# Two output norms that give their rate behind the projection, a sum of squares on GpSimd, and a re-stepped preparation of RWKV

## The reference, cut to what matters

```
h = x
y_ssm = _s5_group(u, ...)          # ends in y * sigmoid(y @ w_glu + b_glu), y = gelu(...)
y_mla = _mla_group(...)            # 8 heads of softmax attention, o of width 1024
y = concatenate([_rmsnorm(y_ssm, ssm_out_norm_w), _rmsnorm(y_mla, mla_out_norm_w)])
h = h + y @ w_out
h = h + _conv_ffn(_rmsnorm(h, ffn_norm_w), ...)
# second layer, RWKV-7 part, before the scan
kk = k * k_k;  kk = kk / max(sqrt(sum(kk * kk, per head)), 1e-12)
k = k * (1 + (a - 1) * k_a)
# _rmsnorm(y, w) = y * rsqrt(mean(y * y) + eps) * w
```

## Time and profile before

| | us |
|---|---|
| median of 3 runs | 3262.21 (3261.06 to 3263.58) |
| the profiled execution | 3260.85 |
| its span | 3258.3 |
| PE busy | 2999.6 (92%) |
| DVE busy | 2159.4 (66%) |
| ACT busy | 1560.1 (48%) |
| POOL busy | 661.4 (20%) |

### The profile page before, as it was taken

One profiled execution on the slowest core, in us unless ns is written; L12 is line 12 of the kernel. 1 busy time (PEld: TensorE's weight loads), 2 busy tenths in 40 slices (PEclk: granted clock), 3 DMA queues, 4 the chain that ended last, 5 costly groups with the idle time before them and its releaser, 6 DMA issues.

```text
span 3258.3 us, 49703 instructions
## 1 busy us (share of the span) xinstructions
PE 2999.6 (92%) x19690; PEld 2659.3 (82%) x19690; DVE 2159.4 (66%) x3555; ACT 1560.1 (48%) x2542; POOL 661.4 (20%) x829
## 2 busy tenths in 40 slices
PE   5876899999999997899999999898899999999998
PEld 4864778888888887888888888776788888888887
DVE  8787778775777656766666666665666665566655
ACT  3334455554555544455555555444544444344443
POOL 5234102110112000764444440000100111001100
PEclk8987999999999998999999999998999999999999
DMA  4410445556555554322222223432364555655554
GB/s 180 152 65 23 159 143 185 190 175 192 203 194 188 166 176 162 127 72 85 82 85 84 73 82 101 154 112 78 130 203 172 191 186 174 194 201 192 193 167 144
DMA packets 78804, 475.13 MB, mean 146 GB/s; under 512 B 8113, under 2 KB 11185, under 8 KB 37425
## 3 DMA queue, kind: packets, MB, share of 16 engines
q1 hardware_dynamic: 76480, 459.66, 41.4%
q10 hardware_dynamic: 2096, 12.32, 1.1%
HBM read 465.66 MB, written 6.29 MB: 145 GB/s over the span
## 4 chain that ended last, share of the span: by engine, by line
PE 75%; DVE 14%; ACT 6%; issue 2%; POOL 2%; DMA 1%; DVEq 0%; ACTq 0%; SPq 0%
PE bank L684 35%; PE bank L688 22%; PE bank L686 4%; PE bank L687 4%; DVE m L1165 3%; ACT m L1979 2%; PE bank L700 2%; DVE m L1809 1%; PE bank L977 1%; POOL m L2599 1%; POOL m L2603 1%; PE bank L978 1%; PE bank L865 1%; PE bank L974 1%; PE bank L980 1%
## 5 line engine op out<-in xcount | busy, mean ns | idle before, releaser
L688 PE MATMUL bank<-m,m 128*128 128x256 f32 x6864 | 1939.7, 283 | 0.0
L684 PE MATMUL bank<-m,m 128*128 128x512 f32 x4992 | 1757.3, 396 | 17.1 <-POOL m L2478 10.2
L1165 DVE TENSOR_TENSOR m<-m,m 128x1024 fp32r<-128x1024 f32 (+1 forms) x944 | 1077.1, 1149 | 630.6 <-ACT m L1979 616.5
L688 PEld LDWEIGHTS bank<-m,m 128*128 128x128 f32 x6864 | 1311.5, 191 | 1.6
L1979 ACT ACTIVATE m<-m 128x1024 fp32r<-128x1024 f32 (+1 forms) x944 | 912.5, 979 | 786.0 <-PE bank L688 734.8
L684 PEld LDWEIGHTS bank<-m,m 128*128 128x128 f32 x4992 | 941.0, 189 | 231.1 <-issue 14.6
L686 PE MATMUL bank<-m,m 128*128 128x256 f32 x1872 | 573.7, 306 | 77.7 <-DVE m L1165 68.8
L687 PE MATMUL bank<-m,m 128*128 128x256 f32 x1872 | 541.1, 289 | 0.0
L686 PEld LDWEIGHTS bank<-m,m 128*128 128x128 f32 x1872 | 370.4, 198 | 107.5 <-issue 89.2
L687 PEld LDWEIGHTS bank<-m,m 128*128 128x128 f32 x1872 | 371.1, 198 | 3.3 <-issue 1.9
L2580 POOL TENSOR_TENSOR m<-m,m 128x256 fp32r<-128x256 f32 x44 | 63.4, 1441 | 695.6 <-ACT m L2180 695.6
(11 more groups left out here) (361 smaller groups left out, 3018.0 us busy)
## 6 DMA issues: line engine op xcount, KB each, us to landing
m<-in_w_up SPq DMA_DIRECT2D x88, 1024.0 KB, 4.9
m<-in_w_down SPq DMA_DIRECT2D x128, 704.0 KB, 4.0
m<-in_w_gu SPq DMA_DIRECT2D x88, 1024.0 KB, 4.9
m<-in_w_out SPq DMA_DIRECT2D x48, 1024.0 KB, 5.1
m<-in_w_krv SPq DMA_DIRECT2D x48, 1024.0 KB, 4.9
m<-in_w_xbc SPq DMA_DIRECT2D x24, 1024.0 KB, 4.9
m<-in_w_z SPq DMA_DIRECT2D x16, 1024.0 KB, 4.9
m<-in_w_in SPq DMA_DIRECT2D x14, 1024.0 KB, 5.0
```

The costliest lines, as they stand in the source:

```text
L684: pe.matmul(bank.rearrange("p (a b) -> p a b", a=2), hi, x, start=kc == L.k0, stop=False)
L688: m = pe.matmul(ps, lo, x[:, 0, :], start=False, stop=last)
L1165: v.tensor_tensor(lo_of(k), raw_of(k)[0], hi_of(k).bitcast(F32), SUB).then_inc(*lo_v(("lo", k)))
```

## The change

1. The norms of the heads (`N_mla`) and of the state space (`N_ssm`) become `late`: ACT cuts weight·chunk high, DVE low; DVE's `rated` multiplies each output tile by the rate (into `xb3`) and adds it to h, two DVE instructions as before. POOL squares and adds the chunks (`sum_squares`), inside the heads and inside GLU, and PE sums over the partitions once (`add_total`). L_out and L_out2 are no longer wide.
2. `o` and `vt` change places in h, and x comes back in two loads of 1 MB, h[:, 0:8] and h[:, 8:16].
3. Seven of the eight cuts of y go into L_out's odd tiles, and all low parts of y to POOL.
4. S5's setup: PE's transposes and k0 products, and ACT's copies of them, stand earlier.
5. RWKV's `prep` has seven steps instead of five or six: the exponentials are a step apart, the root comes ahead of `ka`, `spread`, DVE's `ka` product and DVE's last step are later, and one of the two empty rounds between the preparation and the solve goes.

```diff
@@ -448,8 +450,8 @@
-        o = h[:, 0:8, :]
-        vt = h[:, 8:16, :].rearrange("p (a b) c -> p a (b c)", a=2)
+        o = h[:, 8:16, :]
+        vt = h[:, 0:8, :].rearrange("p (a b) c -> p a (b c)", a=2)
@@ -556,9 +558,9 @@
-        L_out = linear("w_out", 16, 16, TWO, lambda t: res_v["mla", t], k0=8, wide=True)
+        L_out = linear("w_out", 16, 16, TWO, lambda t: res_v["mla", t], k0=8)
...
-        L_out2 = linear("w_out", 16, 16, FOUR, lambda t: res_v["ssm", t], k1=8, wide=True)
+        L_out2 = linear("w_out", 16, 16, FOUR, lambda t: res_v["ssm", t], k1=8)
@@ -604,9 +606,10 @@
-        N_mla = Norm(norms, [o[:, i, :] for i in range(8)], ("mla_out_norm_w", 0), hn_out[8:16], 1024, 1e-6, 2)
+        N_mla = Norm(norms, [o[:, i, :] for i in range(8)], ("mla_out_norm_w", 0), hn_out[8:16], 1024, 1e-6, 2,
+                     late=True)
...
-                     [(ssr[:, 0, i, :], ssr[:, 1, i, :]) for i in range(8)], 1024, 1e-6, 7)
+                     [(ssr[:, 0, i, :], ssr[:, 1, i, :]) for i in range(8)], 1024, 1e-6, 6, late=True)
@@ -623,6 +626,10 @@
+        def total_of(N):
...
+            return sqb if N is N_mla else (spare, xb3[2])
@@ -704,6 +711,11 @@
+            def add_total(N):
+                pe.wait_ge(*(mla_g if N is N_mla else glu_g)["sum", 7])
+                pe.matmul(banks[N.bank][:, 0:T], ones, total_of(N)[0], start=True, stop=True).then_inc(
+                    *sum_pe((N.id,)))
@@ -718,7 +730,7 @@
-                for _ in range(7):
+                for _ in range(5):
@@ -727,7 +739,7 @@
                             m.then_inc(*s5_pe(("abT", r, c // 4)))
-                for _ in range(6):
+                for _ in range(5):
                     yield
@@ -893,8 +905,10 @@
                 yield
+                yield
                 pe.wait_ge(*wkv_a["rn", i])
                 spread(b, rn4[e]).then_inc(*wkv_pe(("rn", i)))
+                yield
                 yield
@@ -1113,13 +1126,17 @@
-            run(linear(L_glu, nrhs,
-                       lambda kc: [glu_a["yhi", kc], (glu_g if kc % 2 else glu_v)["ylo", kc]],
+            run(linear(L_glu, nrhs, lambda kc: [glu_a["yhi", kc], glu_g["ylo", kc]],
...
-            add_squares(N_ssm)
...
+            def out2(t):
+                if t == 0:
+                    add_total(N_ssm)
+                sums_(t)
...
-                       free=[[glu_a["s", 4 + n]] for n in range(4)], done=sums_))
+                       free=[[glu_a["s", 4 + n]] for n in range(4)], done=out2))
@@ -1212,7 +1229,7 @@
-                v.wait_ge(*norm_pe["sq", N.q0 + N.nk - 1])
+                v.wait_ge(*(sum_pe[N.id,] if N in (N_mla, N_ssm) else norm_pe["sq", N.q0 + N.nk - 1]))
@@ -1265,6 +1282,20 @@
+                return done
...
+            def rated(N, *key):
...
+                def done(t):
+                    L, n = key[-1], key[:-1]
+                    x = xb3[t % 2]
+                    v.wait_ge(*lin_pe["tile", L.number(t)])
+                    v.wait_ge(*norm_a["rr", N.id])
+                    v.wait_ge(*res_v.last)
+                    v.tensor_tensor(x, banks[L.banks[t % len(L.banks)]][:, 0:T], rl, MUL).then_inc(*res_v())
+                    v.wait_ge(ld_x2[t // 8], 16)
+                    v.wait_ge(*res_v.last)
+                    v.tensor_tensor(h[:, t, :], h[:, t, :], x, ADD).then_inc(*res_v((*n, t)))
@@ -1520,10 +1551,10 @@
-                norm(N_mla)
-                v.wait_ge(ld_x2, 16)
-                yield
-                yield from linear(L_out, residual("mla", L_out))
+                for i in range(8):
+                    low(N_mla)(i)
+                yield from rate(N_mla)
+                yield from linear(L_out, rated(N_mla, "mla", L_out))
@@ -1660,15 +1691,17 @@
                 v.reciprocal(rn[:, :, 0:2], rn[:, :, 0:2]).then_inc(*wkv_v(("rn", i)))
-                v.wait_ge(*wkv_a["ka", i])
-                v.tensor_tensor(s1, s4, KK(i), MUL).then_inc(*wkv_v(("ka", i)))
                 yield
...
                 yield
+                v.wait_ge(*wkv_a["ka", i])
+                v.tensor_tensor(s1, s4, KK(i), MUL).then_inc(*wkv_v(("ka", i)))
+                yield
                 v.wait_ge(*wkv_pe["rn", i])
+                v.wait_ge(*wkv_v["ka", i])
                 v.scalar_tensor_tensor(out=s4, in0=KK(i), scalar=W("rwkv_k_k_2", i), in1=b[:, 0:T], op0=MUL,
@@ -1908,18 +1940,16 @@
-            for i in range(0, 8, 2):
-                v.wait_ge(*glu_a["yhi", i])
-                v.tensor_tensor(hnr[:, 1, i, :], y[:, i, :], hnr[:, 0, i, :].bitcast(F32), SUB).then_inc(
-                    *glu_v(("ylo", i)))
...
-            run(linear(L_glu, glu))
-            norm(N_ssm, glu_v.last)
-            out = Lag(L_out2, residual("ssm", L_out2), lambda t: None, low(N_ffn))
+            gates = Lag(L_glu, glu, low(N_ssm))
+            run(linear(L_glu, gates))
+            gates.tail()
+            out = Lag(L_out2, rated(N_ssm, "ssm", L_out2), lambda t: None, low(N_ffn))
+            run(rate(N_ssm, glu_v.last))
@@ -2031,16 +2061,16 @@
             def s5_ab():
-                for _ in range(8):
-                    yield
-                yield from s5_tables(0)
+                for _ in range(5):
+                    yield
                 for r in range(2):
...
                                      banks[4 + 2 * r + n][:, :], ACT.Copy).then_inc(*s5_a(("abT", r, n)))
-                for _ in range(6):
-                    yield
+                for _ in range(3):
+                    yield
+                yield from s5_tables(0)
@@ -2107,15 +2137,23 @@
+                a.wait_ge(*mla_pe["o", 15])
+                a.dma_start(h[:, 0:8, :], d["xT"][:, 0:8, :]).then_inc(ld_x2[0], 16)
+                a.wait_ge(*mla_a["o", 15])
...
-                    square(N_mla, i, mla_a["o", 2 * i + 1])
-                norm(N_mla)
-                a.wait_ge(*norm_v["x", N_mla.x0 + 7])
+                    high(N_mla, i)
+                a.wait_ge(*norm_v["lo", N_mla.x0 + 7])
...
-                a.wait_ge(*mla_pe["o", 15])
-                a.dma_start(h, d["xT"]).then_inc(ld_x2, 16)
-                yield
-                yield from linear(L_out, lambda t: None)
+                a.wait_ge(*mla_g["sum", 7])
+                a.dma_start(h[:, 8:16, :], d["xT"][:, 8:16, :]).then_inc(ld_x2[1], 16)
+                yield from rate(N_mla)
...
+                def cut_y(t):
+                    if t < 14 and t % 2:
+                        a.wait_ge(*s5_a["y", t // 2])
+                        a.activation(hnr[:, 0, t // 2, :], y[:, t // 2, :], ACT.Copy).then_inc(*glu_a(("yhi", t // 2)))
...
+                yield from linear(L_out, cut_y)
@@ -2245,16 +2283,18 @@
                              scale=-math.exp(-0.5)).then_inc(*wkv_a())
+                yield
                 a.wait_ge(*wkv_a.last)
                 a.activation(s3, s3, ACT.Exp, scale=math.exp(-0.5)).then_inc(*wkv_a(("pi", i)))
+                yield
+                a.wait_ge(*wkv_v["rn", i])
+                a.activation(rn[:, :, 0:2], rn[:, :, 0:2], ACT.Sqrt).then_inc(*wkv_a(("rn", i)))
                 yield
...
                 yield
-                a.wait_ge(*wkv_v["rn", i])
-                a.activation(rn[:, :, 0:2], rn[:, :, 0:2], ACT.Sqrt).then_inc(*wkv_a(("rn", i)))
                 yield
@@ -2400,11 +2438,15 @@
-            run(linear(L_glu, glu))
-            for i in range(8):
-                square(N_ssm, i, glu_v["y2", i], glu_v["y2", 7])
-            norm(N_ssm)
+            def weighted(t):
+                a.wait_ge(*glu_v["y2", t])
+                high(N_ssm, t)
...
+            gates = Lag(L_glu, glu, weighted)
+            run(linear(L_glu, gates))
+            gates.tail()
...
+            run(rate(N_ssm))
@@ -2557,10 +2599,30 @@
+            def sum_squares(sig, N, i):
+                total, sq = total_of(N)
+                g.tensor_tensor(sq if i else total, N.chunks[i], N.chunks[i], MUL).then_inc(*sig())
+                g.wait_ge(*sig.last)
+                if i:
+                    g.tensor_tensor(total, total, sq, ADD).then_inc(*sig(("sum", i)))
+                    g.wait_ge(*sig.last)
...
+            def head(i):
+                for _ in range(5):
+                    yield
+                if i % 2:
+                    g.wait_ge(*mla_a["o", i])
+                    sum_squares(mla_g, N_mla, i // 2)
...
+            def cut_y(t):
+                if t < 14 and t % 2:
+                    g.wait_ge(*glu_a["yhi", t // 2])
+                    g.tensor_tensor(hnr[:, 1, t // 2, :], y[:, t // 2, :], hnr[:, 0, t // 2, :].bitcast(F32),
+                                    SUB).then_inc(*glu_g(("ylo", t // 2)))
...
-                norm(N_mla)
-                yield
-                yield from linear(L_out)
+                yield
+                yield from linear(L_out, cut_y)
@@ -2640,14 +2701,16 @@
-            heads = flight(lambda i: iter(range(5)), 16, 4)
```

(33 more changed lines are left out.)

## The result

The changed kernel takes 3191.0 us (median of 4 runs, 3188.41 to 3193.0), the kernel before 3262.57 beside it: a ratio of 0.9781, 95% interval 0.9764 to 0.9798. The forecast was 3194. The span went from 3258.3 to 3187.6 us, PE's busy share from 92% to 93%, its mean clock from 0.964 to 0.975.

A forecast was written before the change was run, and what follows sets the result against it. Most of the span was taken to be PE's, with DVE pacing the heads; gains were PE's stops and slow clock after them. Terms summed to −68.6 us against 3260.85, 3192.3, plus 1.4 for the median: 3194, range 3178 to 3212.

The forecast's parts named there:

- RWKV, −37: RWKV's preparation: PE's 29.2 us of waits for ACT's root and 14 of slow clock, 85% of it gained, −37 us.
- up to a round late once, 4.3 us: RWKV's solve: DVE's later final step, if free DVE time did not hide it, delays the solve once, 4.3 us.
- Rival A: RWKV: PE's wait only moves, to the same place or the solve; gain 5 instead of 37, 3226 us, chance 0.17.
- The heads, +6: Attention heads: POOL's squares and adds delay DVE's scan in three of four groups, a loss of 6 us.
- the scan starts at 288.0, 1.9 us later: Heads: square, add and c1 on POOL after ACT's late copy delay DVE's scan from 286.06, by 1.9 us.
- rival B: Heads: POOL's sums cost more, 4.1 us a group and 16.4 in four, giving 3204 us; chance 0.14.
- MLA's half and GLU, −20.0: Heads' norm and its w_out half, −14.9 us by earlier blocks; GLU, −5.1 by moving cuts of y into w_out.
- The rate behind the first tiles: MLA's half of w_out: reciprocal, root and product come late, ahead of freeing one of two banks, +1.2 us.
- The SSM half, −13.6: State space's half of w_out: blocks start right at GLU's end and tile 0 runs faster, −13.6 us.
- The setup, −4: S5's setup: PE's transposes and k0 products come earlier, shortening waits between PE and DVE, −4 us.
- Narrow blocks, +1.2: Both w_out halves: three products of 256 columns per block cost 0.005 us more each, +0.6 us per half.
- Three signs: Profile after: PE's busy share about 94%, DVE's heads scans waiting 3 to 7 us for POOL, w_out starting within 2 us.

The follow-up runs named there:

- e1: The changed kernel with RWKV's preparation as before in all four programs: 3228.1 us, ratio 0.9898.
- e2: The changed kernel with PE's spread back one round earlier, all else as changed: 3216.43 us, ratio 0.986.
- e3: The changed kernel with ACT's root back behind ka, the spread at its new, later round: 3217.15 us, ratio 0.9865.
- e8: The changed kernel with the heads' squares on ACT, summed by eight products of PE, the rate still late: 3190.28 us, ratio 0.9775.
- e10: The changed kernel with the whole cut of y behind the mixer, on ACT, DVE and POOL as before: 3194.29 us, ratio 0.9795.
- e9: The changed kernel with x in one load of 2 MB, issued where the second half is issued: 3192.1 us, ratio 0.9784.
- e12: The changed kernel with the state space's norm done before its half of w_out, as it was, blocks still narrow: 3203.18 us, ratio 0.982.
- e4: The changed kernel with S5's setup in its old places: 3195.01 us, ratio 0.9794.
- e11: The kernel before with both halves of w_out narrow and one DVE addition per tile, nothing else changed: 3263.7 us, ratio 1.0004.
- e6: The changed kernel with all eight POOL sums behind the last head instead of inside the heads: 3198.09 us, ratio 0.9802.
- e5: The changed kernel with a second, unread square and add per chunk on POOL in the heads: 3203.07 us, ratio 0.9813.
- e7: The changed kernel with each group's POOL sums just behind c1 instead of ahead of it: 3191.67 us, ratio 0.9782.

## Why the prediction was right

- **RWKV, −37**: measured −36.2 between the roots, 37 by e1. The mechanism was the one forecast, and its sum, but not where it falls: between the first three roots nothing was gained (120.6 us against 120.9), in the next block 5.5 and in the four steady ones 7.6 each instead of 5.65. Two things that the sum left out offset each other, and that is luck: smaller waits of PE shrank from 3.6 to 1.8 us a block, and in the second block the wait moved to the solve (4.02 us), which the prediction named as a danger ("up to a round late once, 4.3 us") and counted with nothing. That the root ahead of `ka` adds much cover of its own was wrong: in e2 it took 0.7 us off the wait of a steady block, and e2 and e3 show that the round between root and spread decides. Rival A is out but for that one block: PE's waits for the same two steps of the scan on DVE are 11.5 us in all (L1789 10.8, L1782 0.7), and were 12.3 before (L1756 3.2, L1749 9.1).
- **The heads, +6**: this term failed in its size; +0.2 between the marks, 0.5 in each of two groups. The step that failed is "the scan starts at 288.0, 1.9 us later", taken as lost in full in three groups. I took a group in which ACT's copies came late, with PE at 2.93 us for products that took 1.60 in the first two groups, and I took DVE to be idle until c1. It had its own instructions there. The scan does start 1.5 us later, as these are slower beside the sums, and 0.9 of it comes back behind the scan. That is rival B's mechanism at an eighth of its price, 0.53 instead of 4.1 us a group. By the rule of the Trainium skill that the prediction named for this, SBUF — State Buffer, section Who interferes with whom, the trace agrees: L1479, with two inputs in SBUF, took 0.95 us beside L2607 and 0.42 alone.
- **MLA's half and GLU, −20.0**: measured −20.3. Of its parts, from the last group of heads to the first gate of GLU, e8 gives the single sum 4.0 us, e10 the cut of y 4.9 of 5.1 (3.3 in the time), e9 the two loads 1.4 (1.1 in the time, which is not told from nothing). The rate behind the first tiles cost PE 0.54 us, not 1.2.
- **The SSM half, −13.6**: −12.6, and 12.2 by e12.
- **The setup, −4**: 4.0 by e4, 2.6 at N_q's mark.
- **Narrow blocks, +1.2**: e11's +2 us is not told from nothing.

The total was nearer than its terms, which is luck too: the heads' error of 5.8 us was against RWKV's 0.8, the SSM half's 1.0 and the setup's 1.4, and against 0.9 us at the end. The range was added up wrong: from its terms as they stand it is 3181 to 3215, not 3178 to 3212; 3191.0 lies in both.

Three signs that the prediction named did not come. PE's busy share rose to 93.1%, not about 94%: PE's busy time fell as well, from 2999.6 to 2969.1 us, in part since the same products run at the higher clock. DVE's scans waited 2.7 us in all for POOL in the heads, as before (2.8), not 3 to 7. And the first block of w_out came 3.5 us behind the end of the last head on PE (301.08), not within 2.

One thing stays open. What an edit of the first layer costs there is not all in the time: from the last sums of the SSM half to the end of the span it is 2750.5 us in the changed kernel and 2746.5 in e8, 2747.1 in e6, 2747.9 in e5, with the same program behind. In e8 the 4 us are spread: 1.0 up to the first RWKV root, 0.9 between the roots, 2.1 behind the last. In e4, e7, e9, e10 and e12 it is 2747.5 to 2749.6 us, so the changed kernel's trace is the longest of nine. Four executions of the changed kernel differ by 4.6 us themselves, so it may be nothing but that; no run tells.

## What to carry to other kernels

A norm whose rate is applied to the outputs of the projection takes the whole chain of squares, reciprocal, root and weighting off the path (12 us for the norm of the state space, measured by e12). For the heads' norm it made no difference to the time whether POOL or PE summed the squares (e8). Where engines run fixed programs, count the rounds between a producer's step and its consumer's: in the same round PE waited for everything that ACT does ahead of it, with one round between, in the steady blocks, for nothing. A later round for one step can make the next one late, as at the second solve. Before a wait is priced from one row, see whether the waiting engine was idle there in the other periods as well.
